# Gate products of an MLP in matmuls of 256 columns instead of 512, and part of the up products

## The reference, cut to what matters

```python
        h2 = rms_norm(x, norm2_g[layer]) * (1 + sc2[:, None]) + sh2[:, None]
        ff = (jax.nn.silu(h2 @ w_gate[layer]) * (h2 @ w_up[layer])) @ w_down[layer]
        x = x + g2[:, None] * ff
    return rms_norm(x, final_g)
```

## Time and profile before

| | us |
|---|---|
| timed, median of 2 | 2396.08 |
| timed, lowest and highest | 2393.58, 2398.58 |
| span of the profiled execution | 2399.9 |
| PE busy | 2327.5 (97%) |
| PEld busy | 1888.4 (79%) |
| DVE busy | 1193.5 (50%) |
| ACT busy | 708.5 (30%) |
| POOL busy | 233.7 (10%) |

### The profile page before, as it was taken

One profiled execution on the slowest core, in us unless ns is written; L12 is line 12 of the kernel. 1 busy time (PEld: TensorE's weight loads), 2 busy tenths in 40 slices (PEclk: granted clock), 3 DMA queues, 4 the chain that ended last, 5 costly groups with the idle time before them and its releaser, 6 DMA issues.

```text
span 2399.9 us, 29138 instructions
## 1 busy us (share of the span) xinstructions
PE 2327.5 (97%) x10280; PEld 1888.4 (79%) x10280; DVE 1193.5 (50%) x1600; ACT 708.5 (30%) x986; POOL 233.7 (10%) x211
## 2 busy tenths in 40 slices
PE   7999999989998998999999999999999999999997
PEld 5878888766776886888888888888888888888885
DVE  7877777776777888322332222333222333222234
ACT  4234333455444113222222222222222222222221
POOL 3012333000004331000000000000000000000032
PEclk8999999999999999999999999999999999999998
DMA  9796666523433983222233222233222233222232
GB/s 333 267 355 170 198 199 199 164 98 126 147 122 113 346 293 123 96 90 102 81 96 111 96 95 97 81 97 111 96 96 96 84 98 107 96 96 96 86 96 106
DMA packets 120058, 333.75 MB, mean 139 GB/s; under 512 B 11897, under 2 KB 36617, under 8 KB 119505
## 3 DMA queue, kind: packets, MB, share of 16 engines
q1 hardware_dynamic: 115282, 318.03, 39.5%
q0 software_dynamic: 3728, 15.01, 2.7%
q10 hardware_dynamic: 1008, 0.21, 0.1%
HBM read 325.55 MB, written 7.65 MB: 139 GB/s over the span
## 4 chain that ended last, share of the span: by engine, by line
PE 87%; DVE 7%; DMA 3%; ACT 1%; issue 1%; SPq 0%; DVEq 0%; ACTq 0%
PE P L435 18%; PE P L437 18%; PE P L436 18%; PE T L435 9%; PE T L436 9%; PE T L437 9%; DMA att<-in_w_ada 1%; DVE W_lo L1037 1%; DVE rstd L1123 1%; DMA adar<-in_w_ada 1%; PE T L498 1%; PE S L480 1%; ACT W_hi L705 1%; DVE att L1072 1%; DVE att L1310 1%
## 5 line engine op out<-in xcount | busy, mean ns | idle before, releaser
L435 PE MATMUL P<-H_hi,W_hi 128*128 128x512 f32 x2112 | 841.6, 398 | 22.3 <-DVE H_lo L1325 10.3
L1037 DVE TENSOR_TENSOR W_lo<-raw,W_hi 128x1024 fp32r<-128x1024 f32 (+2 forms) x416 | 475.1, 1142 | 723.1 <-ACT W_hi L705 719.7
L436 PE MATMUL P<-H_lo,W_hi 128*128 128x512 f32 x2112 | 826.9, 392 | 0.0
L437 PE MATMUL P<-H_hi,W_lo 128*128 128x512 f32 x2112 | 826.8, 391 | 0.0
L705 ACT ACTIVATE W_hi<-raw 128x1024 fp32r<-128x1024 f32 (+2 forms) x416 | 406.2, 977 | 1054.5 <-PE P L437 562.8
L435 PEld LDWEIGHTS P<-H_hi,W_hi 128*128 128x128 f32 x2112 | 398.8, 189 | 120.6 <-issue 29.2
L437 PEld LDWEIGHTS P<-H_hi,W_lo 128*128 128x128 f32 x2112 | 399.0, 189 | 84.6
L436 PEld LDWEIGHTS P<-H_lo,W_hi 128*128 128x128 f32 x2112 | 399.1, 189 | 80.7 <-issue 1.9
L435 PE MATMUL T<-F_hi,W_hi 128*128 128x512 f32 x704 | 273.9, 389 | 0.0
L436 PE MATMUL T<-F_lo,W_hi 128*128 128x512 f32 x704 | 273.9, 389 | 0.0
L437 PE MATMUL T<-F_hi,W_lo 128*128 128x512 f32 x704 | 273.9, 389 | 0.0
(11 more groups left out here) (175 smaller groups left out, 1695.8 us busy)
## 6 DMA issues: line engine op xcount, KB each, us to landing
raw<-in_w_gu SPq DMA_DIRECT2D x176, 512.0 KB, 3.2
raw<-in_w_in SPq DMA_DIRECT2D x72, 512.0 KB, 4.4
adar<-in_w_ada SPq DMA_DIRECT2D x72, 512.0 KB, 4.2
att<-in_w_ada SPq DMA_DIRECT2D x32, 1024.0 KB, 9.0
att<-in_w_ada SPq DMA_DIRECT2D x56, 512.0 KB, 4.9
raw<-in_w_down SPq DMA_DIRECT2D x64, 384.0 KB, 3.1
raw<-in_w_down SPq DMA_DIRECT2D x64, 320.0 KB, 2.8
raw<-in_w_out SPq DMA_DIRECT2D x32, 512.0 KB, 4.9
```

Of the source, the lines that this page charges most:

```text
L435: pe.matmul(bank[:, :], wh, xh, start=start, stop=False)
L436: pe.matmul(bank[:, :], wh, xl, start=False, stop=False)
L437: return pe.matmul(bank[:, :], wl, xh, start=False, stop=stop)
L1037: dve.tensor_tensor(lo[:, 0:cols], raw[:, raw_slot * PW:raw_slot * PW + cols], hi[:, 0:cols].bitcast(F32), ALU.subtract).then_inc(lo_done, 1)
```

## The change

In `gate_up` the gate product now uses `half_tile`: each block's three products are done for columns 0 to 255 and then for columns 256 to 511 of the bank, six matmuls of 256 columns. The up product uses `low_half_tile`: the two products with the high weight stay at 512 columns, the one with the low weight becomes two of 256. A start flag stands only on the first matmul into a bank. Operands, results, semaphores, DMAs and the work of the other engines are the same. The first step (`pair`) and the down products keep `tile`.

```diff
+HS = S // 2
...
-            def piece(n, slot, bank, src_hi, src_lo, kts, last_k, between=()):
+            def piece(n, slot, bank, src_hi, src_lo, kts, last_k, between=(), tile=tile):
...
+            def half_tile(bank, w, j, src_hi, src_lo, k, start, stop):
+
+                wh, wl = w[0][:, j * P:j * P + P], w[1][:, j * P:j * P + P]
+                for t in range(2):
+                    out = bank[:, t * HS:t * HS + HS]
+                    xh, xl = src_hi[:, k * S + t * HS:k * S + t * HS + HS], src_lo[:, k * S + t * HS:k * S + t * HS + HS]
+                    pe.matmul(out, wh, xh, start=start and t == 0, stop=False, skip_group_check=True)
+                    pe.matmul(out, wh, xl, start=False, stop=False, skip_group_check=True)
+                    mm = pe.matmul(out, wl, xh, start=False, stop=stop and t == 1, skip_group_check=True)
+                return mm
+
+            def low_half_tile(bank, w, j, src_hi, src_lo, k, start, stop):
+
+                wh, wl = w[0][:, j * P:j * P + P], w[1][:, j * P:j * P + P]
+                xh, xl = src_hi[:, k * S:k * S + S], src_lo[:, k * S:k * S + S]
+                pe.matmul(bank[:, :], wh, xh, start=start, stop=False, skip_group_check=True)
+                pe.matmul(bank[:, :], wh, xl, start=False, stop=False, skip_group_check=True)
+                for t in range(2):
+                    mm = pe.matmul(bank[:, t * HS:t * HS + HS], wl, src_hi[:, k * S + t * HS:k * S + t * HS + HS],
+                                   start=False, stop=stop and t == 1, skip_group_check=True)
+                return mm
...
-                        piece(n0 + 4 * f + (2 * g + h), h, Pb[g], H_hi, H_lo, half_kts(h), KT - 1)
+                        piece(n0 + 4 * f + (2 * g + h), h, Pb[g], H_hi, H_lo, half_kts(h), KT - 1,
+                              tile=low_half_tile if g else half_tile)
```

## The result

The changed kernel takes 2437.1 us (median) against 2396.1: the ratio is 1.0168 with a 95% interval of 1.0149 to 1.0187, that is +41 us (+36 to +45). The profiled execution has a span of 2434.2 us.

What follows compares the result with a forecast made beforehand. TensorE's matmul pace in the MLP was taken to bound the kernel. A fixed 13.3 ns for each of 2752 extra matmuls gave +36.7 us on 2396.1, so 2432.8 us, range 2390 to 2445.

Steps and rivals of the forecast that it cites:

- The bound: In the MLP TensorE is busy without a gap at clock 1.00, so only its matmul pace can move the end.
- 3 us of cover for the weight split: Split weights for the next MLP piece are ready 3 us before they are due, so this costs nothing.
- The count: 64 more matmuls in each of 43 steps of f: 2752 more matmuls and 2752 more loads, 13032 matmuls in all.
- The load: A weight load costs 111 ns uncovered; halves can follow every 111 to 114 ns, so it stays just covered.
- The start-up: In the MLP's halved products, 13.3 ns is paid per matmul instruction: a half takes 120.0 ns, +36.7 us; chance 58%.
- Rival 1: In the halves, the 13.3 ns go with the columns and the load is the floor: about 2400 us; chance 22%.
- the matmul at 953.15 us: After 1.11 us of PE idling it has the same 0.39 us, taken to exclude an effect of the neighbouring load.
- The sum: Whole run: 2396.1 + 36.7 = 2432.8 us timed, +1.5%.
- The step of f: One MLP step grows by 0.85 us, from 21.75 to 22.60 us.
- Rival 2: In the gate halves the load is no longer covered and adds to the start-up: +77 us, 2473 us; chance 14%.

Runs made afterwards that it cites:

- the quarters: Against the kernel before, gate products cut into matmuls of 128 columns, up products unchanged: 2851.9 us, ratio 1.190.
- `gate_only`: Against the kernel before, only the gate products are halved, up products unchanged: 2426.6 us, ratio 1.0128.
- `all_half`: Against the kernel before, gate and up products are both halved in full: 2454.1 us, ratio 1.0246.
- `narrow_load`: Against the kernel before, gate products keep 512 columns but use 64 of 128 stationary columns: MLP +6.4 us.
- `up_alternate`: Against the kernel before, gate products unchanged, the four matmuls of an up block ordered 512, 256, 512, 256: MLP +20.3 us.

## Why the prediction was right, point by point

- **The bound.** That PE's pace alone carries the MLP held: no idle time appeared, clock 1.00, and no other engine's work changed. The 3 us of cover for the weight split were not touched.
- **The count.** 2752 more matmuls and loads, 10280 to 13032.
- **The load.** Priced at 111 to 114 ns from the short sequences of the earlier trace rows; the quarters showed 111.4 over whole products. The load stayed covered in the gate halves.
- **The start-up, the step on which all turned.** Halves at 120.0 ns in the changed kernel, in `gate_only` and in `all_half`: fixed for each instruction. Rival 1 is refuted by the same number. The reason I gave, a reader that has no slack at the full rate, is supported by the packed bfloat16 runs (2.6 ns) and by the pace at the lower clock, but not proved: the load was changed with the stream there, and no run parts a matmul from its load. One argument that I gave for it was none: that the matmul at 953.15 us is recorded with the same 0.39 us says nothing of its pace, as the end of a record is modelled. That a load beside it doesn't take the 13.3 ns rests on `narrow_load` alone.
- **The sum.** Forecast +36.7 us, 2432.8. MLP in the traces +38.9, timed +41.0, with 36 to 45 as its interval. The term that was mis-sized is the up product: I let its 512-column matmuls stay at 226.7 ns and its halves at 120.0, a block of 693.3 ns. It was 696.5, with starts 233 ns apart behind the whole ones and 115 behind the halves. 688 x 3.2 = 2.2 us; 36.7 + 2.2 = 38.9 is the MLP's growth. The remaining 2 us between trace and timing lie within the interval.
- **The step of f.** Forecast 22.60, measured 22.67 us. Of the difference 16 x 3.2 ns = 0.05 us is the up product, the rest is rounding.
- **Rival 2** had 14%. With the floor now measured at 111.4, that was more than its mechanism deserved: load and start-up overlap.

## What to carry to other kernels

When PE is busy back to back, read its pace from the starts, subtract columns / clock, and ask what is left for each instruction: here 13.3 ns for float32r, so a cut of a 512-column matmul in two even halves costs that once. By an estimate from these numbers a part below some 235 columns falls to the 111 ns of load and matmul instead ((111.4 - 13.3) x 2.4 = 235); no run tried a size between 128 and 256. Mixed sizes cost 3 to 12 ns more for each block. A weight load's record (0.19 us) is not its price; look for two loads in close succession. A change that only adds instructions to the engine that bounds the kernel needs no wait to cost time.

## What the runs showed that I had not expected

- Products that mix whole float32r matmuls with halves are slower than the sum of both: 696.5 ns a block in the changed kernel, 705.6 with `up_alternate`, against 693.3. Starts 224 to 240 ns apart also follow on a wait or another type or size, for five to nine matmuls.
- Half as many stationary columns (`narrow_load`) made the pace slower, 229.9 ns, not faster.
- bfloat16 read with a step of two elements runs at 225.3 ns, packed at 216.0: so the type alone does not set the pace (the packed run also had constant data).
